# Hybrid decoder step: four samples' weights ahead of two key units, and value fetches between row fetches

## The chip, the core and the metric

One core of a Trainium2 chip runs the kernel. The metric is the device time of one execution in microseconds; lower is better.

## The reference

One layer of a decoder for 256 prompt tokens and 8 sample tokens (width 1024). After a norm and one projection, two mixers run for each group, then a merge, a router and 32 small experts.

```python
# mixer A, sample: top 256 of 2049 keys by an indexer's score, their K and V rows gathered
score = einsum(relu(q_i . k_i), w_i);  sel = top_k(score, 256)
k_sel, v_sel = cache_k_a[phys, off], cache_v_a[phys, off]
o_a = softmax(q . k_sel + bias[bucket(dist)]) @ v_sel
# mixer B, sample: stick-breaking over all 2048 cached keys, 8 heads of 64
z = q . k;  log_keep = log_sigmoid(-z);  after = reverse_cumsum(log_keep) - log_keep
o_b = exp(log_sigmoid(z) + after) @ v
# both mixers also for the prompt, in two blocks of 128 queries; then
h = x + (g_a * (o_a @ w_proj_a) + g_b * (o_b @ w_proj_b)) @ w_out;  out = h + experts(norm(h))
```

## The kernel before

All engines work in a written order; semaphores tie them together. The change lies in the stage in which the samples' mixer B is finished and mixer A runs.

Mixer B of the samples reads K and V caches in 32 units each. A unit is four rows of each of 128 partitions, 1 MB. GpSimd issues each as an indirect DMA (`fetch`, L547 to L550). VectorE multiplies and sums a key unit (`unit(k)`, L1729, 4.6 us). A "used" unit raises `s_kused` or, for values, `s_vused`. Value unit n goes to one of eight slots: from unit 8 on its fetch waits until unit n - 8 is used (`s_vused` at n - 7); units 4 to 7 go to slots of the key ring and wait for the last four key units.

The weights of stick-breaking come for four samples at a time (q = 0, 1). `softplus_keys(q)` scans, `after_keys(q)` on TensorE and `sample_tot(q)` on ScalarE carry the sums across partitions, `later_keys(q)` on VectorE adds them, and `sample_a(q)` on ScalarE takes the exponential into a zeroed pad (`a_pads`, zeroed by GpSimd for q = 0). TensorE's `values(first, units)` (L1015) then takes four matmuls for each unit; unit 0 waits for `sample_a(0)`, unit 16 for `sample_a(1)` and `sample_wide(0)`.

Mixer A of the samples: VectorE writes the list of the selected rows (`list_rows`), and GpSimd fetches 16 blocks of 128 key rows (64 KB each, `got_k`), then 16 of value rows into the same tiles (`got_v`). `turn_got(g)` transposes the key blocks 4g to 4g + 3 on TensorE and ScalarE copies them; `got_v` of a group waits for that transposition. `sample_logits` needs all 16 key blocks, `values_a` all 16 value blocks. Mixer A of the prompt runs between: `prompt_a_scores(i)`, `prompt_a_logits(i)`, ScalarE's `prompt_a_exp(i)` and `prompt_a_values(i, unit)`, which takes value units of mixer B in between its steps. `prompt_b_logits`, `prompt_b_after` and `prompt_b_values` are mixer B of the prompt.

GpSimd's order before: value units 0 to 3, the zeroing, units 4 and 5, key blocks 0 to 7, unit 6, key blocks 8 to 11, unit 7, key blocks 12 to 15, units 8 and 9, value block 0, and then a unit and a value block in turn up to unit 24 and block 15, and units 25 to 31. SP issues the projection weights when 28 value units are used (L483) and the experts' weights behind that.

Of the kernel before, what the change touches and what calls it, by code (L numbers as in the profile page):

```python
# [25 lines left out]
NS = 8  # L26
# [98 lines left out]
def decoder_step(nc, a, out, CONST_AT):  # L125

    ctx = ExitStack()
    with ctx:
# [60 lines left out]
        LIST = 2 * NS  # L189
        got = temp[:, 10240:12288].rearrange("p (x n) -> p x n", x=LIST)  # L190
# [39 lines left out]
        got_row = pads[:, 743:743 + LIST].bitcast(I32)  # L230
# [102 lines left out]
        s_got_k = [sem(f"s_got_k{i}") for i in range(4)]  # L333
# [50 lines left out]
        ka_rows = a["cache_k_a"][0].rearrange("n s h d -> (n s) (h d)")  # L384
# [160 lines left out]
        @block.gpsimd  # L545
        def _(pool):
            def fetch(dst, src, idx, landed):  # L547

                pool.indirect_dma_start(out=dst, out_offset=None, in_=src,  # L549
                                        in_offset=bass.IndirectOffsetOnAxis(ap=idx, axis=0)).then_inc(landed, 16)  # L550

            def fetch_k(k):
                b, u = k // 4, k % 4
                fetch(k_ring[:, u].rearrange("p r n -> p (r n)"), kb_rows, unit_idx[:, u, b:b + 1], s_k[u])

            def fetch_v(n):
                if n >= 8:
                    pool.wait_ge(s_vused, n - 7)
                elif n >= 4:
                    pool.wait_ge(s_kused, 4 * NS - 7 + n)  # L560
                fetch(v_slot(n).rearrange("p r n -> p (r n)"), vb_rows, unit_idx[:, n % 4, n // 4:n // 4 + 1], s_v[n % 8])

            def got_k(g):
                for x in range(4 * g, 4 * g + 4):
                    fetch(got[:, x, :], ka_rows, got_row[:, x:x + 1], s_got_k[g])

            def got_v(x):
                if x % 4 == 0:
                    pool.wait_ge(s_tr, M_GOT + x // 4 + 1)
                fetch(got[:, x, :], va_rows, got_row[:, x:x + 1], s_got_v)  # L570

            pool.wait_ge(s_ms, 1)
            nc.gpsimd.tensor_tensor(rstd, ms, const("half"), ALU.pow).then_inc(s_rstd, 1)
            pool.wait_ge(s_idx, 4)
            pool.wait_ge(s_wa, 16)
            for g in range(2):
                for k in (2 * g, 2 * g + 1):
                    fetch_k(k)
                for b in range(4 * g, 4 * g + 4):
                    fetch(kidx_ring[:, b, :], kidx_rows, page_idx[:, b:b + 1], s_kidx[g])  # L580
            for k in range(4, 4 * NS):
                pool.wait_ge(s_kused, k - 3)
                fetch_k(k)
            pool.wait_ge(s_proj, N_ALL)
            for n in range(4):
                fetch_v(n)
            nc.gpsimd.memset(a_pads[0], 0.0).then_inc(s_apad0, 1)
            fetch_v(4)
            fetch_v(5)
            pool.wait_ge(s_rows, 1)  # L590
            got_k(0)
            got_k(1)
            fetch_v(6)
            got_k(2)
            fetch_v(7)
            got_k(3)
            for n in range(8, 4 * NS):
                fetch_v(n)
                if 9 <= n < 9 + LIST:
                    got_v(n - 9)  # L600

            for n, t in enumerate((0, 2, 1)):
                pool.wait_ge(s_ms2, n + 1)
                nc.gpsimd.tensor_tensor(rstd[:, t:t + 1], ms[:, t:t + 1], const("half")[:, t:t + 1], ALU.pow  # L604
                                        ).then_inc(s_rstd2, 1)

            for t in range(3):
                pool.wait_ge(s_ms3, t + 1)
                nc.gpsimd.tensor_tensor(rstd[:, t:t + 1], ms[:, t:t + 1], const("half")[:, t:t + 1], ALU.pow  # L609
                                        ).then_inc(s_rstd3, 1)  # L610

        @block.tensor
        def _(pe):
# [211 lines left out]
            def turn_got(g):  # L825
                m = M_GOT + g
                pe.wait_ge(s_got_k[g], 64)
                pe.wait_ge(s_trf, m - 1)
                for k in range(4):
                    last = nc.tensor.transpose(PS[:, 2 + m % 2, k * P:(k + 1) * P], got[:, 4 * g + k, :], ident)  # L830
                last.then_inc(s_tr, 1)
# [183 lines left out]
            def values(first, units):  # L1015

                for k in range(first, first + units):
                    b, u, q = k // 4, k % 4, k // 16
                    if k % 16 == 0:
                        pe.wait_ge(s_as, q + 1)  # L1020
                    if k == 16:
                        pe.wait_ge(s_owide, 1)
                    pe.wait_ge(s_v[k % 8], k // 8 * 16 + 16)
                    for r in range(4):
                        last = nc.tensor.matmul(PS[r * 32:(r + 1) * 32, 0, :], a_pad[q][:, b % 4, 4 * u + r, :],  # L1025
                                                v_slot(k)[:, r, :], start=(k % 16 == 0), stop=(k % 16 == 15))
                    last.then_inc(s_vused, 1)
# [8 lines left out]
                last.then_inc(s_tr, 1)  # L1036

            prompt_a_logits(0)
            values(0, 3)
            turn_got(0)  # L1040
            turn_got(1)
            prompt_a_scores(1)
            values(3, 2)
            turn_got(2)
            turn_got(3)
            sample_logits()
            values(5, 1)
            after_keys(1)
            prompt_a_values(0, 6)
            prompt_a_logits(1)  # L1050
            values(10, 2)
            turn_soft()
            prompt_a_turn(0)
            values(12, 2)
            prompt_b_logits(0)
            values(14, 2)
            prompt_a_values(1, 16)
            fold_heads(0)
            prompt_a_turn(1)
# [240 lines left out]
        def _(act):  # L1300
# [113 lines left out]
            def sample_a(q, s_zero):  # L1414
                act.wait_ge(s_zero, 1)
                act.wait_ge(s_ts, q + 1)
                nc.scalar.activation(a_own[q], z_s[:, 4 * q:4 * q + 4, :].rearrange("p b (h r) -> p b r h", r=R), ACT.Exp  # L1417
                                     ).then_inc(s_as, 1)
# [25 lines left out]
            def list_told(m, dst):  # L1444
                act.wait_ge(s_tr, m + 1)
                nc.scalar.copy(dst, PS[:, 2 + m % 2, 0:dst.shape[1]]).then_inc(s_trf, 1)
# [14 lines left out]
            sample_tot(0)  # L1461
            act.wait_ge(s_tr, M_NEW + 1)
            nc.scalar.copy(tmp64, PS[0:64, 2 + M_NEW % 2, 0:NS]).then_inc(s_trf, 1)
            list_told(M_BUCKET, bucketT)
            def turned_got(g):
                m = M_GOT + g
# [70 lines left out]
                                          PS[half, 1 if k == 0 else ACC + 3, :].rearrange("p (c q) -> p c q", c=2))  # L1537
                last.then_inc(s_obT, 1)

            sample_a(0, s_apad0)  # L1540
            sample_ln(1)
            prompt_a_exp(0)
            turned_got(0)
# [132 lines left out]
        def _(dve):  # L1676
# [274 lines left out]
            unit(13 + ROUNDS)  # L1951
            softplus_keys(0)
            list_rows()
            unit(14 + ROUNDS)
            unit(15 + ROUNDS)
            later_keys(0)
            link(nc.vector.tensor_scalar(wi_scaled, wi_rows[:, :, :], float(H ** -0.5 * HD ** -0.5), None, ALU.mult))

            def prompt_a_scores(i):
# [397 lines left out]
```

## Time and profile before

| | us |
|---|---|
| median of 3 runs (667.5 to 670.08) | 667.61 |
| profiled execution | 666.25 |
| its span | 664.4 |
| TensorE busy | 562.7 |
| VectorE busy | 371.5 |
| GpSimd busy | 129.8 |
| ScalarE busy | 136.2 |

The span is the time from the first to the last instruction; the rest of the profiled execution's time lies around it. Busy time of an engine is a share over all stages and tells little of the stage at hand. There the share of the 16 transfer engines and the granted TensorE clock (1.00 is 2.4 GHz, 0.50 is 1.2 GHz) are to be read by stretches.

### The profile page before, as it was taken

To read this page: it belongs to the slowest core of one execution; us is meant where nothing else is said; L and a number is where in the kernel's file an instruction comes from. 1 tells how busy PE (TensorE), PEld (TensorE's weight loads), DVE (VectorE), ACT (ScalarE), POOL (GpSimd) and SP (SyncE) were. 2 spreads that over 40 slices of the span, in tenths; PEclk is the share of its full clock that TensorE was granted. 3 is DMA by queue.
4 is the path that set the end of the run, shared out by engine and by line. 5 is a ranking of instruction groups with operands and counts; after the bars stand their busy time and mean duration, and the time that the engine had idled before them with its cause. 6 is when DMAs were issued, how large, how long until landed. Compare 5 with 4: busy or idle time off the path is not lost.

```text
span 664.4 us, 7517 instructions
## 1 busy us (share of the span) xinstructions
PE 562.7 (85%) x2900; PEld 317.7 (48%) x2900; DVE 371.5 (56%) x679; ACT 136.2 (20%) x267; POOL 129.8 (20%) x116
## 2 busy tenths in 40 slices
PE   3998889989999467988979997797998989788882
PEld 1775567877888424446468445332322323222220
DVE  4069999999999998820423144734342442414124
ACT  3013401115211144451610021110101111010102
POOL 1625441111111877772000000000000000000001
PEclk9999989999999567985999999798999999999997
DMA  8999768798874948999469983469999999999951
GB/s 311 398 357 334 288 235 325 291 402 299 289 281 133 378 153 314 422 423 394 172 163 408 384 340 106 148 220 417 419 420 418 421 420 421 420 420 421 407 233 68
DMA packets 66318, 213.83 MB, mean 322 GB/s; under 512 B 15379, under 2 KB 17955, under 8 KB 58092
## 3 DMA queue, kind: packets, MB, share of 16 engines
q1 hardware_dynamic: 52108, 137.46, 53.2%
q0 software_dynamic: 11392, 73.41, 28.8%
q10 hardware_dynamic: 2784, 2.51, 1.1%
q8 instruction: 21, 0.34, 0.2%
q14 instruction: 13, 0.11, 0.0%
HBM read 208.76 MB, written 4.60 MB: 321 GB/s over the span
## 4 chain that ended last, share of the span: by engine, by line
PE 44%; DVE 24%; SPq 10%; DMA 7%; ACT 6%; issue 5%; POOL 3%; ACTq 1%; DVEq 0%
PE PS L619 7%; SPq L469 7%; DVE arena L1734 6%; PE PS L1185 6%; DVE x_rows L1738 6%; PE PS L1167 5%; PE PS L1080 4%; PE PS L1095 4%; PE PS L1193 3%; DMA arena<-in_w_down 3%; SPq L474 3%; PE PS L1233 3%; DMA arena<-in_w_up 2%; POOL arena L549 2%; POOL temp L549 1%
## 5 line engine op out<-in xcount | busy, mean ns | idle before, releaser
L619 PE MATMUL PS<-xT,arena 128*128 128x264 f32 x608 | 145.6, 399 | 0.8 <-ACT arena L1376 0.5
L619 PEld LDWEIGHTS PS<-xT,arena 128*128 128x128 f32 x608 | 116.8, 195 | 26.4 <-issue 4.7
L1734 DVE TENSOR_TENSOR arena<-arena,x_rows 128x2048 f32<-128x2048 f32 x32 | 73.1, 2283 | 21.2 <-ACT x_rows L1328 21.1
L1738 DVE TENSOR_REDUCE x_rows<-arena 128x32 f32<-128x2048 f32 x32 | 73.2, 2287 | 1.1
L549 POOL DMA_INDIRECT arena<-in_cache_k_b,unit_idx x32 | 44.6, 1395 | 138.9 <-DVE x_rows L1738 134.5
L1193 PE MATMUL PS<-temp 128*128 128x512 f32 (+1 forms) x96 | 48.9, 646 | 12.4 <-DVE temp L2261 8.1
L1185 PE MATMUL PS<-arena,temp 128*32 128x512 f32 x384 | 48.0, 644 | 9.3 <-DMA arena<-in_w_up 4.8
L609 POOL TENSOR_TENSOR small<-small,consts 128x1 f32<-128x1 f32 x3 | 2.6, 868 | 241.2 <-DVE small L2297 241.2
L2237 DVE TENSOR_TENSOR x_rows<-PS,x_rows 128x512 f32<-128x512 f32 (+1 forms) x48 | 32.9, 687 | 24.4 <-PE PS L1193 24.3
L549 POOL DMA_INDIRECT arena<-in_cache_v_b,unit_idx x32 | 34.9, 1090 | 29.6 <-PE PS L1025 13.4
L2261 DVE COPY temp<-PS 128x512 f32<-128x512 f32 x8 | 5.5, 691 | 55.1 <-PE PS L1233 55.1
L1193 PEld LDWEIGHTS PS<-temp 128*128 128x128 f32 (+1 forms) x96 | 12.8, 164 | 48.3 <-DVE x_rows L2237 25.5
L1185 PEld LDWEIGHTS PS<-arena,temp 128*32 128x32 f32 x384 | 12.0, 118 | 40.8 <-issue 32.3
L1233 PE MATMUL PS<-arena,temp 128*32 128x512 f32 x256 | 29.0, 592 | 0.7 <-DMA arena<-in_w_down 0.7
L1095 PE MATMUL PS<-temp,xT 128*128 128x512 f32 x64 | 28.5, 599 | 0.0
L1025 PE MATMUL PS<-arena,xT 128*32 128x512 f32 x128 | 18.1, 685 | 9.2 <-ACT xT L1417 9.2
L1316 ACT COPY arena<-PS 128x264 f32<-128x264 f32 x22 | 8.3, 378 | 84.9 <-PE PS L619 84.9
L2257 DVE TENSOR_TENSOR temp<-PS,temp 128x256 f32<-128x256 f32 x8 | 3.4, 424 | 35.0 <-ACT temp L1628 35.0
L2220 DVE COPY temp<-PS 128x512 f32<-128x512 f32 x8 | 5.5, 691 | 28.0 <-PE PS L1167 28.0
L549 POOL DMA_INDIRECT temp<-in_cache_k_a,pads x16 | 19.1, 1196 | 4.9 <-issue 4.9
L604 POOL TENSOR_TENSOR small<-small,consts 128x1 f32<-128x1 f32 x3 | 1.6, 548 | 92.4 <-DVE small L2074 76.2
L1167 PE MATMUL PS<-rows_vb,temp 128*128 128x512 f32 x32 | 18.9, 675 | 0.7 <-DVE temp L2194 0.7
(374 smaller groups left out, 804.2 us busy)
## 6 DMA issues: line engine op xcount, KB each, us to landing
arena<-in_w_down SPq DMA_DIRECT2D x32, 1024.0 KB, 15.9
arena<-in_w_gate SPq DMA_DIRECT2D x48, 512.0 KB, 13.1
arena<-in_w_up SPq DMA_DIRECT2D x48, 512.0 KB, 13.6
arena<-in_w_in SPq DMA_DIRECT2D x9, 2048.0 KB, 11.3
temp<-in_w_gate SPq DMA_DIRECT2D x12, 512.0 KB, 14.8
temp<-in_w_up SPq DMA_DIRECT2D x12, 512.0 KB, 14.7
temp<-in_w_out SPq DMA_DIRECT2D x1, 4096.0 KB, 15.3
x_rows<-in_x_prompt SPq DMA_DIRECT2D x2, 1024.0 KB
```

What stands on the lines that cost most here:

```text
L469: sp.dma_start(region[:, g * 4 * DE:(g + 1) * 4 * DE], w[e].rearrange("o (p h c) f -> h (o p) (c f)", p=P, h=2)[half]).then_inc(s_second i ...
L549: pool.indirect_dma_start(out=dst, out_offset=None, in_=src, in_offset=bass.IndirectOffsetOnAxis(ap=idx, axis=0)).then_inc(landed, 16)
L619: last = nc.tensor.matmul(PS[0:m, n % 2, 0:T], w[:, k, c0:c0 + m], xT[:, k, :], start=(k == 0), stop=(k == KC - 1))
L1080: last = nc.tensor.matmul(PS[:, bank + c % 2, 0:T], w[:, k, c * P:(c + 1) * P], o[:, k, :], start=(k == 0), stop=(k == 3))
L1095: last = nc.tensor.matmul(PS[:, (6 + 2 * t + n) % 8, :], mixT[:, k, t * P:(t + 1) * P], w_o[:, k, n * 512:(n + 1) * 512], start=(k == 0), ...
L1167: last = nc.tensor.matmul(PS[:, half, :], into[0:n, t, :], x2_rows[t][0:n, half * 512:(half + 1) * 512], start=(t == 0), stop=(t == 2))
L1185: last = nc.tensor.matmul(PS[k * CAP:(k + 1) * CAP, 2, :].rearrange("p (g f) -> p g f", g=2), xgT[:, d, k * CAP:(k + 1) * CAP], both[:, :, ...
L1193: return nc.tensor.matmul(PS[0:n, ACC + 2 + half, :], backT[:, t0:t0 + n], y_sb[:, half, :], start=True, stop=True)
L1233: last = nc.tensor.matmul(PS[k * CAP:(k + 1) * CAP, ACC + half, :], hidT[:, f, k * CAP:(k + 1) * CAP], slots[k][:, w0:w0 + 512], start=(f ...
L1734: nc.vector.tensor_tensor(k_ring[:, u], k_ring[:, u], q_all[:, b % 2:b % 2 + 1, :].to_broadcast([P, 4, H * HD]), ALU.mult).then_inc(s_mul, 1)
L1738: nc.vector.tensor_reduce(z_s[:, b, :].rearrange("p (h r) -> p r h", r=R)[:, 4 * u:4 * u + 4, :], k_ring[:, u].rearrange("p r (h d) -> p r ...
L2237: nc.vector.tensor_tensor(x_rows[0:n, t, cols], PS[0:n, ACC + 2 + half, :], x_rows[0:n, t, cols], ALU.add).then_inc(added, 1)
```

## The change

VectorE runs `later_keys(0)` in front of key units 30 and 31. ScalarE runs `sample_a(0)` in front of its copy of the buckets. GpSimd issues key blocks 0 to 3, then units 6, 8, 9, 7, 10 to 15, each followed by one key block, then key blocks 14 and 15; from unit 16 on value blocks follow, two behind each of units 16 to 19 and one behind each of units 20 to 27. TensorE takes value units 0 to 5 at once, 6 and 7 behind `turn_got(0)`, 8 behind `turn_got(1)` and `prompt_a_scores(1)`, 9 behind `sample_logits`, 10 to 13 within `prompt_a_values(0)`, and 14 and 15 singly behind it.

```diff
--- before.py
+++ after.py
@@ -560,9 +560,8 @@
                     pool.wait_ge(s_kused, 4 * NS - 7 + n)
                 fetch(v_slot(n).rearrange("p r n -> p (r n)"), vb_rows, unit_idx[:, n % 4, n // 4:n // 4 + 1], s_v[n % 8])
 
-            def got_k(g):
-                for x in range(4 * g, 4 * g + 4):
-                    fetch(got[:, x, :], ka_rows, got_row[:, x:x + 1], s_got_k[g])
+            def got_k(x):
+                fetch(got[:, x, :], ka_rows, got_row[:, x:x + 1], s_got_k[x // 4])
 
             def got_v(x):
                 if x % 4 == 0:
@@ -588,16 +587,20 @@
             fetch_v(4)
             fetch_v(5)
             pool.wait_ge(s_rows, 1)
-            got_k(0)
-            got_k(1)
-            fetch_v(6)
-            got_k(2)
-            fetch_v(7)
-            got_k(3)
-            for n in range(8, 4 * NS):
+            for x in range(4):
+                got_k(x)
+            for x, n in enumerate((6, 8, 9, 7, 10, 11, 12, 13, 14, 15)):
                 fetch_v(n)
-                if 9 <= n < 9 + LIST:
-                    got_v(n - 9)
+                got_k(4 + x)
+            got_k(14)
+            got_k(15)
+            for n in range(16, 4 * NS):
+                fetch_v(n)
+                if n < 20:
+                    got_v(2 * n - 32)
+                    got_v(2 * n - 31)
+                elif n < 28:
+                    got_v(n - 12)
 
             for n, t in enumerate((0, 2, 1)):
                 pool.wait_ge(s_ms2, n + 1)
@@ -1036,24 +1039,24 @@
                 last.then_inc(s_tr, 1)
 
             prompt_a_logits(0)
-            values(0, 3)
+            values(0, 6)
             turn_got(0)
+            values(6, 2)
             turn_got(1)
             prompt_a_scores(1)
-            values(3, 2)
+            values(8, 1)
             turn_got(2)
             turn_got(3)
             sample_logits()
-            values(5, 1)
+            values(9, 1)
             after_keys(1)
-            prompt_a_values(0, 6)
+            prompt_a_values(0, 10)
             prompt_a_logits(1)
-            values(10, 2)
+            values(14, 1)
             turn_soft()
             prompt_a_turn(0)
-            values(12, 2)
+            values(15, 1)
             prompt_b_logits(0)
-            values(14, 2)
             prompt_a_values(1, 16)
             fold_heads(0)
             prompt_a_turn(1)
@@ -1461,6 +1464,7 @@
             sample_tot(0)
             act.wait_ge(s_tr, M_NEW + 1)
             nc.scalar.copy(tmp64, PS[0:64, 2 + M_NEW % 2, 0:NS]).then_inc(s_trf, 1)
+            sample_a(0, s_apad0)
             list_told(M_BUCKET, bucketT)
             def turned_got(g):
                 m = M_GOT + g
@@ -1537,7 +1541,6 @@
                                           PS[half, 1 if k == 0 else ACC + 3, :].rearrange("p (c q) -> p c q", c=2))
                 last.then_inc(s_obT, 1)
 
-            sample_a(0, s_apad0)
             sample_ln(1)
             prompt_a_exp(0)
             turned_got(0)
@@ -1951,9 +1954,9 @@
             unit(13 + ROUNDS)
             softplus_keys(0)
             list_rows()
+            later_keys(0)
             unit(14 + ROUNDS)
             unit(15 + ROUNDS)
-            later_keys(0)
             link(nc.vector.tensor_scalar(wi_scaled, wi_rows[:, :, :], float(H ** -0.5 * HD ** -0.5), None, ALU.mult))
 
             def prompt_a_scores(i):
```

## Rows read from the trace of the kernel before

**Rows 1.** Chain that ended last: start us, us, what.

```profile
268.12 0.94 POOL arena L549
...
293.97 7.49 DMA temp<-in_cache_v_a,pads
```

**Rows 2.** Five stretches: columns us, engines' busy (instructions), PEclk, DMA share, GB/s.

```profile
232.00:253.00 21.00, 11.22 (x69) 4.68 (x70) 18.54 (x52) 11.69 (x27) 15.82 (x18) 0.74 0.47 153
253.00:315.00 62.00, 54.63 (x357) 33.41 (x357) 29.69 (x60) 21.49 (x50) 40.02 (x38) 0.81 1.00 406
...
285.00:286.00 1.00, 1.00 (x8) 0.08 (x8) 0.00 (x0) 0.30 (x1) 0.76 (x1) 0.50 0.99 418
...
301.50:314.50 13.00, 13.00 (x43) 10.46 (x44) 0.00 (x0) 1.95 (x5) 2.19 (x3) 0.50 1.01 414
329.90:333.60 3.70, 3.67 (x12) 2.13 (x13) 1.76 (x1) 1.32 (x2) 0.00 (x0) 1.00 1.01 411
```

**Rows 3.** Timeline, VectorE: start us, us, instruction, [idle before it <- releaser].

```profile
224.71 2.28 DVE L1734 TENSOR_TENSOR arena<-arena,x_rows 128x2048 f32<-128x2048 f32 x1
...
233.75 0.20 DVE L1926 TENSOR_TENSOR small<-pads,x_rows 128x32 f32<-128x32 f32 x1
233.98 0.69 DVE L1929 TENSOR_TENSOR x_rows<-x_rows,small 128x512 f32<-128x512 f32 x1
...
270.07 2.48 DVE L1980 SCALAR_TENSOR_TENSOR temp<-PS,temp 128x512 f32<-128x512 f32 x4 [1.12 <-PE PS L931]
```

**Rows 4.** Timeline, GpSimd: four of its issues.

```profile
225.18 2.63 POOL L549 DMA_INDIRECT temp<-in_cache_k_a,pads  x1 [0.30 <-issue]
...
233.88 0.95 POOL L549 DMA_INDIRECT temp<-in_cache_k_a,pads  x1 [0.30 <-issue]
...
250.13 1.24 POOL L549 DMA_INDIRECT temp<-in_cache_k_a,pads  x1 [0.30 <-issue]
...
293.97 2.35 POOL L549 DMA_INDIRECT temp<-in_cache_v_a,pads  x1 [0.31 <-issue]
```

**Rows 5.** Timeline, ScalarE: `sample_tot(0)`, bucket copy, `sample_a(0)` with its table load.

```profile
221.57 0.18 ACT L1412 COPY pads<-PS 128x32 f32<-128x32 f32 x1 [1.49 <-PE PS L783]
...
226.00 0.58 ACT L1446 COPY temp<-PS 128x512 f32<-128x512 f32 x1 [3.43 <-PE PS L821]
234.75 1.28 ACT L1417 ACT_TABLE_LOAD   x1 [8.17 <-DVE x_rows L1929]
236.04 1.07 ACT L1417 ACTIVATE xT<-x_rows 128x512 f32<-128x512 f32 x1
```

**Rows 6.** Timeline, TensorE.

```profile
225.89 2.08 PE L931 MATMUL PS<-arena 64*128 64x128 f32 x16
237.17 5.35 PE L1025 MATMUL PS<-arena,xT 128*32 128x512 f32 x24 [9.20 <-ACT xT L1417]
...
252.94 0.75 PE L830 MATMUL PS<-consts,temp 128*128 128x128 f32 x4 [0.49 <-DMA temp<-in_cache_k_a,pads]
255.19 1.09 PE L840 MATMUL PS<-temp,bias_b 128*64 128x128 f32 x4 [1.50 <-ACT obT L1468]
...
283.49 1.46 PE L961 MATMUL PS<-rows_kva,temp 128*128 128x64 f32 x8 [2.39 <-ACT temp L1507]
...
292.97 1.07 PE L1025 MATMUL PS<-arena,temp 128*32 128x512 f32 x8
...
295.44 2.78 PE L1025 MATMUL PS<-arena,temp 128*32 128x512 f32 x24
301.50 0.68 PE L864 MATMUL PS<-pads,rows_kva 8*128 8x64 f32 x2 [3.27 <-DMA temp<-in_cache_v_a,pads]
302.11 7.00 PE L867 MATMUL PS<-pads,temp 128*128 128x8 f32 x32
```

**Rows 7.** Issues of 250 to 251 and of 251.5 to 252.5 us, us to landing.

```profile
temp<-in_cache_k_a,pads POOLq DMA_INDIRECT x1, 2.8
...
arena<-in_cache_v_b,unit_idx POOLq DMA_INDIRECT x1, 5.4
```

## The prediction, on record before the result

> **What bounds the kernel now.** I read the chain of waits first, then the share of the transfer engines by stretch, then the timelines of GpSimd, VectorE, ScalarE and TensorE between 220 and 342 us, and last the landing times of the indirect fetches.
>
> The reader is to see one stage, from about 225 to 341 us, in which GpSimd issues 32 value units of 1 MB, 16 blocks of key rows and 16 blocks of value rows (64 KB each) one after the other. An issue takes 0.94 us and the next follows 0.30 us later, so one per 1.25 us [rows 4]. The chain runs over these issues from 268 to 294 us and ends in the landing of the last block of value rows, 7.49 us after its issue began [rows 1]. TensorE has reached `values_a` by then: its last value units before it end at 295.44 + 2.78 = 298.2, and it stands 3.27 us until 301.5 [rows 6]. From 232 to 253 us the transfer engines are only 0.47 busy, so 21 x 0.53 = 11 us of their time are lost; from 253 to 315 they are full [rows 2]. The change aims at that gap. But the order in which GpSimd issues also says when the sixteen blocks of key rows are there, and TensorE, which works in a written order, waits for them before `sample_logits`.
>
> **Weights earlier (VectorE, ScalarE).** `later_keys(0)` now stands at 233.75, behind two key units of which the first begins at 224.71 [rows 3]. What it needs, `sample_tot(0)`, is done at 221.57 + 0.18 [rows 5]. So it runs at 224.7 without a wait and takes 0.9 us, and both key units end 0.9 us later; VectorE's work is only reordered and its next step starts as before. On ScalarE `sample_a(0)` moves ahead of the copy at 226.00; its table load of 1.28 us and the activation of 1.07 us, now 234.75 to 237.1 [rows 5], come to 225.7 to 228.1. The copy then runs at 228.1 instead of 226.0; its consumers are VectorE's `prompt_a_logits(0)` (243.9, not late) and `sample_logits`. TensorE finishes `prompt_a_logits(0)` at 225.89 + 2.08 = 228.0, so its first value unit starts at 228.1 instead of 237.17, 9 us earlier [rows 6]. That alone shortens nothing, because another wait stands behind it.
>
> **Fetches reordered (GpSimd).** Counted in issues from 225.18: before, the last block of key rows is the 18th (16 blocks and units 6 and 7) and begins at 250.13 [rows 4]. After, it is the 26th: four blocks, ten pairs of unit and block, two blocks. None of the units 6 to 15 waits for its slot: unit 8 needs one used unit and comes at 236.4, and unit 7 needs the last key unit, done at 234.7, and comes at 241.4. The first four blocks are as before and end at 233.88. From there 21 issues lie ahead of it, 233.88 + 21 x 1.25 = 260.1, 10.0 us later than now.
>
> Its landing: before, with the engines half empty, 2.8 us after the issue, 252.9 [rows 7]. After, ten units and twelve blocks stand in the queue from 235.3 on, with no idle engine between. A unit is 1.05 MB, at about 420 GB/s 2.5 us; a block some 0.3 us (from 253 to 315 us 23 units and 16 blocks passed: 23 x 2.5 + 16 x 0.3 = 62.3 [rows 2]). 10 x 2.5 + 12 x 0.3 = 28.6, so 263.9, and 1 us for completion: 264.9. Ends: 262.9 if it lands 2.8 us after its issue as now, and 266.5 if it has the 7.5 us of the last value rows less their long issue.
>
> The Trainium skill, "DMA: Bandwidth & Descriptors", section "Anatomy of one DMA", gives a DMA issued from GpSimd as 2.0 us and its bytes over 436 GB/s; for 64 KB an estimate of 2.15 us, near the 2.8 us measured in the half empty stretch, far from the 7.49 us in the full one. By that formula alone the block would land at 262.3 and the sum below would be 2.6 us less.
>
> **What that does to TensorE.** Values(6, 2) and `turn_got(1)` wait for unit 7 and block 7 until about 248; `prompt_a_scores(1)` then ends at about 252.5, when ScalarE is free for it anyway, so this costs nothing. `turn_got(3)` runs at 264.9 instead of 252.94. With 0.75 us for its transposes, 0.6 us for the copy and the signals, `sample_logits` starts at 266.6 instead of 255.19 [rows 6]: 11.4 us late (9.4 to 13 by the ends above).
>
> Behind it all is serial. Five value units and `prompt_a_values(0)` lie between `sample_logits` and `prompt_a_logits(1)`, before and after alike; VectorE waits for the latter today, 1.12 us [rows 3], then forms logits and maximum, ScalarE's exponentials follow, and TensorE waits 2.39 us for ScalarE's copies at 283.49 [rows 6]. Four units fewer stand between `sample_logits` and that point now, but TensorE has slack there, and so the 3.8 us of them (1.92 us for two) buy nothing. So TensorE arrives at `values_a` at 298.2 + 11.4 = 309.6.
>
> The value rows: GpSimd's unit 17 needs ten used units, and the tenth is computed after `sample_logits`, at 272; GpSimd could have issued at 265.1 and stands 7 us, and the engines run dry about as long, so most of the 11 us gained is lost again. The last block of value rows now stands behind unit 27, before behind unit 24; unit 27 needs twenty used units, the last of which ends at 292.97 + 1.07 + 11.4 = 305.4 [rows 6]. Unit 27 is issued at 305.6, the block at 306.9. The engines have caught up by then, so unit 27 lands after 5.4 us [rows 7], at 311, and the block with it. `values_a` starts at 311.0: 3.3 us of wait shrink to 1.4, and the stage is 9.5 us late (7.8 to 11.4 by the two ends).
>
> **The clock.** Before, TensorE's granted clock is 0.50 (1.2 GHz) from the wait at 298.2 through `values_a` and `prompt_b_after(0)`, 13.0 us of work; `prompt_b_after(1)`, the same matmuls, takes 3.7 us at 1.00 (2.4 GHz) [rows 2] where the first took 6.5. With the wait cut to 1.4 us, the clock may stay up for a part. All of it would give 3.5 us (half of the 7.0 of `values_a`) and 2.8 us, 6.3 in all; nothing is the other end. The wait of 2.39 us before 283.49 was followed by a fall (0.50 at 285) [rows 2, 6], and `values_a` streams eight columns a matmul [rows 6], light work, so I take 1.5 us, nearer to nothing.
>
> The Trainium skill, "TensorE: Matmul & The Clock Gate", section "HAM oscillation", advises to finish the matmuls of a group before the next wait for a transfer, so that the engine stays at 2.4 GHz; the change does that with six units and then two. By that rule the whole 6.3 us would come back, the rival "clock" below. The trace agrees in so far as the clock was down behind the two waits of 2.39 and 3.27 us [rows 2, 6]; no row shows what a wait of 1.4 us does.
>
> **Sum.** The rest of the stage, the weights of the projections (issued when 28 units are used) and the experts follow TensorE, so the delay passes to the end. 666.25 us of the profiled execution + 9.5 - 1.5 = 674.25. The median of the three runs, 667.61, lies 1.36 above the profiled one: **675.5 us**.
>
> **Rivals.**
> *Clock:* all as above, but the clock stays at 2.4 GHz through `values_a` and `prompt_b_after(0)`. For it speaks the shorter wait, against it the light matmuls. +9.5 - 6.3: 670.8 us.
> *Catch-up (the other side):* the engines' 11 us are won and `sample_logits` is not late, since the key rows pass the units in the queue. It decides from a delay of `sample_logits` under 3.3 us, the present wait at `values_a`. Then only the issues count: the last value rows are three later, 293.97 + 3.75 = 297.7, land 2.8 us later at 300.5, 1.0 us earlier than now, and the clock stays up: 667.6 - 1.0 - 6.3 = 660.3 us. Against it: the 26th issue cannot begin before 260.1.
> *Weights not early:* the table load or the zeroing of the pad holds `sample_a(0)`, the first value unit still starts at 237, and unit 8 waits for its slot until 239, 2.5 us longer than forecast. Everything behind is later by that, 678.1 us. The zeroing stands ahead of the key rows on GpSimd, which speaks against it.
> *Queue:* key rows at the late end and unit 27 later: +11.4 and no clock: 679.0 us.
>
> **How the numbers follow.** Forecast 0.62, clock 0.14, catch-up 0.07, weights not early 0.05, queue 0.12. The range goes from the early end of the delay with the full clock (+7.8 - 6.3, 669.1) to +11.4 with none (679.0): 669.5 to 679. About 0.5% (3.3 us) is what a measurement of this kernel can tell from no change. Faster by more: the catch-up case, 0.06. Within: the rest of it and the half of the clock case under 670.9, with the lowest edge of the forecast, 0.09. Slower: 0.85.
>
> **What would show it.** Right: the first value unit on TensorE at 228; the last key-row issue at about 260 and `turn_got(3)` waiting on it until 264 to 266; a gap of some 7 us in GpSimd's issues behind unit 16; `sample_logits` 9 to 13 us later; the wait ahead of `values_a` under 2 us. Wrong: `sample_logits` before 259, or transfer engines full from 235 to 300 without a gap.

## The result, and the profile after

The changed kernel takes 683.97 us (median of 4 runs, 682.37 to 684.74), the kernel before beside it 667.56 us (4 runs, 665.04 to 670.08). The ratio is 1.024 with an interval of 1.020 to 1.029: slower by 16.4 us. I had forecast 675.5 us and a range up to 679.0. The direction was right, the size was too small by half (some 8 us of the 16.4), and the time lies outside the range.

The profiled execution took 684.74 us with a span of 682.9 us and a mean granted clock of 0.915. Lines of the changed kernel stand 3 lines lower from the reordered part on (L1025 is now L1028, L864 is L867). This execution was 1.83 us ahead at the first value fetch on GpSimd, before anything of the change acts (212.22 against 214.05 us). So a delay within the stage is the time after, plus 1.83, minus the time before.

First the five columns of stretches, as in [rows 2], of the changed kernel: start:end, us, busy time of PE, PEld, DVE, ACT and POOL with instructions, PEclk, DMA share, GB/s.

```profile
232.00:253.00 21.00, 9.27 (x52) 4.36 (x56) 17.19 (x51) 9.82 (x26) 16.12 (x17) 0.67 0.96 376
253.00:315.00 62.00, 42.92 (x293) 25.02 (x285) 29.04 (x59) 19.49 (x44) 37.82 (x37) 0.77 0.78 286
```

The gap is filled as it was meant to be: the transfer engines go from 0.47 to 0.96, a gain of 21 x 0.49 = 10.3 us. But the stretch behind goes from 1.00 to 0.78, a loss of 62 x 0.22 = 13.6 us. TensorE's busy time there falls from 54.63 to 42.92 us. The empty time has moved, and grown.

TensorE's timeline, in the form of [rows 6], shows where:

```profile
226.36 5.52 PE L1028 MATMUL PS<-arena,xT 128*32 128x512 f32 x40 [0.18 <-ACT xT L1420]
...
246.45 1.93 PE L1028 MATMUL PS<-arena,xT 128*32 128x512 f32 x8 [8.17 <-DMA arena<-in_cache_v_b,unit_idx]
...
257.61 1.12 PE L833 MATMUL PS<-consts,temp 128*128 128x128 f32 x4 [3.79 <-DMA temp<-in_cache_k_a,pads]
...
263.61 1.12 PE L833 MATMUL PS<-consts,temp 128*128 128x128 f32 x4 [4.88 <-DMA temp<-in_cache_k_a,pads]
265.49 1.08 PE L843 MATMUL PS<-temp,bias_b 128*64 128x128 f32 x4 [0.77 <-ACT obT L1472]
...
293.27 1.97 PE L964 MATMUL PS<-rows_kva,temp 128*128 128x64 f32 x8 [3.08 <-ACT temp L1511]
...
308.43 2.78 PE L1028 MATMUL PS<-arena,temp 128*32 128x512 f32 x24
...
315.49 0.68 PE L867 MATMUL PS<-pads,rows_kva 8*128 8x64 f32 x2 [4.28 <-DMA temp<-in_cache_v_a,pads]
316.10 7.00 PE L870 MATMUL PS<-pads,temp 128*128 128x8 f32 x32
...
356.14 2.02 PE L1083 MATMUL PS<-oaT,arena 128*128 128x264 f32 x8 [1.25 <-ACT obT L1540]
```

The wait of 9.20 us for the first weights is gone, and the first unit starts at 226.36. In its place stand 8.17 us for unit 6, 3.79 for key rows and 4.88 for the last key rows. `sample_logits` starts at 265.49 + 1.83 = 267.3, 12.1 us later than at 255.19. The wait at `values_a` has not shrunk from 3.27 us, it is 4.28.

GpSimd's timeline, in the form of [rows 4], has the stall behind unit 16, and the issues of units 24 to 27 with the last value-row block (the last key-row block is issued at 258.88):

```profile
271.64 0.94 POOL L549 DMA_INDIRECT arena<-in_cache_v_b,unit_idx  x1 [8.08 <-PE PS L1028]
...
297.41 0.94 POOL L549 DMA_INDIRECT arena<-in_cache_v_b,unit_idx  x1 [2.67 <-PE PS L1028]
...
301.93 0.94 POOL L549 DMA_INDIRECT arena<-in_cache_v_b,unit_idx  x1 [2.32 <-PE PS L1028]
...
305.30 0.94 POOL L549 DMA_INDIRECT arena<-in_cache_v_b,unit_idx  x1 [1.18 <-PE PS L1028]
...
307.79 1.50 POOL L549 DMA_INDIRECT arena<-in_cache_v_b,unit_idx  x1 [0.30 <-issue]
...
309.60 1.49 POOL L549 DMA_INDIRECT temp<-in_cache_v_a,pads  x1 [0.30 <-issue]
```

The chain of waits between 258 and 316 us (start, us, what), which before ran from 268 us on over GpSimd's issues alone [rows 1], now goes through the whole serial part of the stage:

```profile
258.88 4.68 DMA temp<-in_cache_k_a,pads
...
279.86 0.83 DVE temp L1983 x2
...
287.27 2.95 ACT temp L1503 x11
...
293.27 1.97 PE PS L964 x8
...
304.00 1.04 PE PS L1028 x8
...
305.30 0.94 POOL arena L549
...
309.60 5.84 DMA temp<-in_cache_v_a,pads
315.49 0.68 PE PS L867 x2
```

It reads as one story: last key rows, `turn_got(3)`, `sample_logits`, five units with `prompt_a_values(0)`, `prompt_a_logits(1)`, VectorE's logits and maximum, ScalarE's exponentials, `prompt_a_values(1)`, the used slot, unit 26, unit 27, the last value rows, `values_a`.

### The profile page after: what moved, and what is told of

The parts are those of the page before. It is cut to its first block, busy times and chain, and to the rows that moved or that the text cites. A ratio compares the mean times of both kernels' runs of the same rounds, so it can differ in the third digit from the quotient of the medians.

```text
span 682.9 us, 7517 instructions
## 1 busy us (share of the span) xinstructions
PE 571.3 (84%) x2900; PEld 323.2 (47%) x2900; DVE 371.5 (54%) x679; ACT 136.6 (20%) x267; POOL 129.2 (19%) x116
## 4 chain that ended last, share of the span: by engine, by line
PE 50%; DVE 15%; SPq 9%; DMA 9%; ACT 5%; POOL 5%; issue 4%; ACTq 1%; DVEq 0%
PE PS L622 11%; SPq L469 7%; PE PS L1188 6%; PE PS L1170 5%; PE PS L1083 4%; PE PS L1098 4%; DVE arena L1737 4%; DVE x_rows L1741 3%; PE PS L1196 3%; DMA arena<-in_w_down 3%; POOL arena L549 3%; SPq L474 3%; PE PS L1236 3%; DMA arena<-in_w_up 2%; DMA arena<-in_cache_v_b,unit_idx 2%
## 5 line engine op out<-in xcount | busy, mean ns | idle before, releaser
L622 PE MATMUL PS<-xT,arena 128*128 128x264 f32 x608 | 143.3, 394 | 1.1 <-ACT arena L1379 0.7
L1028 PE MATMUL PS<-arena,xT 128*32 128x512 f32 x128 | 17.9, 663 | 12.0 <-DMA arena<-in_cache_v_b,unit_idx 11.8
## 6 DMA issues: line engine op xcount, KB each, us to landing
arena<-in_w_in SPq DMA_DIRECT2D x9, 2048.0 KB, 11.2
temp<-in_w_gate SPq DMA_DIRECT2D x12, 512.0 KB, 13.7
temp<-in_w_up SPq DMA_DIRECT2D x12, 512.0 KB, 13.6
```

Of the source, the lines that this page charges most:

```text
L622: last = nc.tensor.matmul(PS[0:m, n % 2, 0:T], w[:, k, c0:c0 + m], xT[:, k, :], start=(k == 0), stop=(k == KC - 1))
```

## The experiments

The theory after the result (A): the late key rows hold the serial chain back, the late value rows add a part of their own, and TensorE's clock, which falls at the new waits, adds a third part. The rivals: the early weights do the harm, or the order of the units on TensorE does (four fewer units before `prompt_a_values(1)`), or nothing but the clock. The first four kernels, and those at the end, ran where the kernel before took 668 us (the record names chips 13 and 9); a group between them ran where it took 682 to 683 us (chips 11 and 0), and is read against its own runs of the kernel before.

**Early weights alone.** The kernel before with only the two moves:

```diff
+            sample_a(0, s_apad0)
             list_told(M_BUCKET, bucketT)
...
-            sample_a(0, s_apad0)
             sample_ln(1)
...
+            later_keys(0)
             unit(14 + ROUNDS)
             unit(15 + ROUNDS)
-            later_keys(0)
```

> The kernel before with the moves on VectorE and ScalarE alone (later_keys(0) and sample_a(0) early); orders of GpSimd and TensorE as before. Theory A (the order of fetches costs, the early weights cost nothing): first value unit at about 228 instead of 237, end of the stage where it was, 667.6 us within 2. Rival B (the early start itself costs, because TensorE stands longer afterwards and its clock falls in other places): 670 us or more, sample_logits unmoved but more time at 0.50 between 240 and 315 us.

Measured: 668.55 us (10 runs) beside 668.93 of before, ratio 0.9988 (0.996 to 1.0016). TensorE's timeline of it:

```profile
228.63 4.05 PE L1025 MATMUL PS<-arena,xT 128*32 128x512 f32 x24 [0.19 <-ACT xT L1417]
...
240.38 1.12 PE L830 MATMUL PS<-consts,temp 128*128 128x128 f32 x4 [2.81 <-DMA temp<-in_cache_k_a,pads]
...
255.58 0.62 PE L840 MATMUL PS<-temp,bias_b 128*64 128x128 f32 x4 [1.57 <-ACT obT L1469]
...
282.68 1.97 PE L961 MATMUL PS<-rows_kva,temp 128*128 128x64 f32 x8 [2.89 <-ACT temp L1508]
...
296.22 1.08 PE L1034 MATMUL PS<-consts,x_rows 128*128 128x32 f32 x8
```

The wait of 9.2 us goes, waits for the key rows take its place, and `sample_logits` stands where it was (255.58 against 255.19). Harmless and worthless by itself, as forecast. One thing in this profile matters further on: `prompt_a_values(1)` lasts 13.5 us here (282.68 to 296.22, granted clock 0.63) and not the 10.5 us of the profile before (283.49 to 293.97), although TensorE's order is that of before.

**Orders alone.** The changed kernel with those two moves taken back (the diff above, reversed).

> The changed kernel with later_keys(0) and sample_a(0) back in their old places. Theory A: the whole cost of 16 us stays, plus up to 2.5 us because unit 8 waits for its slot until the first unit is used at 239: 684 to 687 us. Rival B: most of the 16 us goes away, under 676 us.

Measured: 688.31 us (4 runs), ratio 1.031 (1.025 to 1.037), 4.3 us over the changed kernel. The intervals overlap, so the 4.3 us are likely rather than settled. `sample_logits` starts at 268.73. So the orders carry the whole loss, and the early weights are, if anything, a help within them. Its `prompt_a_values(1)` is the shorter one, 10.8 us, and yet TensorE waits 3.92 us at `values_a`:

```profile
297.23 1.97 PE L964 MATMUL PS<-rows_kva,temp 128*128 128x64 f32 x8 [2.69 <-ACT temp L1510]
...
308.06 1.08 PE L1037 MATMUL PS<-consts,x_rows 128*128 128x32 f32 x8
...
316.24 0.68 PE L867 MATMUL PS<-pads,rows_kva 8*128 8x64 f32 x2 [3.92 <-DMA temp<-in_cache_v_a,pads]
```

**Key rows first again.** The changed kernel with the key-row blocks where they stood before; TensorE's order and the value rows stay changed.

```diff
-            for x in range(4):
+            for x in range(8):
                 got_k(x)
-            for x, n in enumerate((6, 8, 9, 7, 10, 11, 12, 13, 14, 15)):
+            fetch_v(6)
+            for x in range(8, 12):
+                got_k(x)
+            fetch_v(7)
+            for x in range(12, 16):
+                got_k(x)
+            for n in range(8, 16):
                 fetch_v(n)
-                got_k(4 + x)
-            got_k(14)
-            got_k(15)
```

> The changed kernel with GpSimd's key blocks as before (0 to 7, unit 6, 8 to 11, unit 7, 12 to 15, then units 8 to 15); everything else changed. Theory A (the key rows' place in the queue makes sample_logits 12 us late, and the rest follows): turn_got(3) at about 253, sample_logits at 255, last value rows some 10 us earlier, 668 to 673 us. Rival C (the place of the value rows, behind unit 27 and its wait for used units, sets the time whatever the keys do): 678 us or more.

Measured: 676.56 us (4 runs), ratio 1.0126 (1.0072 to 1.0181): 7.4 us under the changed kernel, with the intervals apart. More was expected. Its timeline says why:

```profile
251.28 1.93 PE L1031 MATMUL PS<-arena,xT 128*32 128x512 f32 x8 [4.50 <-DMA arena<-in_cache_v_b,unit_idx]
...
257.99 1.07 PE L1031 MATMUL PS<-arena,xT 128*32 128x512 f32 x8 [1.27 <-DMA arena<-in_cache_v_b,unit_idx]
260.90 0.62 PE L846 MATMUL PS<-temp,bias_b 128*64 128x128 f32 x4 [0.82 <-ACT obT L1475]
...
308.74 0.69 PE L870 MATMUL PS<-pads,rows_kva 8*128 8x64 f32 x2 [5.89 <-DMA temp<-in_cache_v_a,pads]
```

`sample_logits` comes back only to 260.90, since TensorE's new order puts units 6 to 8 in front of it, and two of them are awaited here (another cost of the change, some 5 us, which the late key rows cover in the changed kernel). The wait at `values_a` grows to 5.89 us: the faster chain meets the same late value rows.

**Value rows earlier.** The changed kernel, last value-row block behind unit 23 instead of 27:

```diff
-                if n < 20:
+                if n < 24:
                     got_v(2 * n - 32)
                     got_v(2 * n - 31)
-                elif n < 28:
-                    got_v(n - 12)
```

> The changed kernel with the last value block behind unit 23 instead of 27 (two blocks behind each of units 16 to 23). Theory A: TensorE still reaches values_a at 311 (its own clock), the wait of 4.3 us there goes, and with it perhaps the fall of the clock: 676 to 680 us. Rival C: under 674 us.

Measured: 679.17 us (4 runs), ratio 1.0162 (1.0106 to 1.0219), 4.8 us under the changed kernel. The two intervals overlap at their edges (the changed kernel's begins at 1.020), but no run of the one reaches the other's (677.25 to 679.71 against 682.37 to 684.74 us). The wait is gone, while `sample_logits` stays late:

```profile
267.76 1.09 PE L841 MATMUL PS<-temp,bias_b 128*64 128x128 f32 x4 [0.77 <-ACT obT L1470]
...
313.57 0.43 PE L865 MATMUL PS<-pads,rows_kva 8*128 8x64 f32 x2
```

**Both given back.** The two last diffs together.

> The changed kernel with both orders given back: key blocks as before, the last value block behind unit 23. Early weights and TensorE's new grouping of value units stay. If the two costs add up (7.4 and 4.8 us found apart), 671 to 673 us; if they overlap, since without the late key rows the wait for the value rows was longer (5.9 us), 668 us or less; if TensorE's grouping costs by itself (units 6 to 9 awaited ahead of key and logit work), it stays above 670 us with sample_logits at 261 instead of 255.

> The same kernel as e8_keys_first_rows_23 once more: there every kernel, the one before too, was some 12 us slower and spread over 15 us, with stretches in which TensorE stood for instructions. Expected as there: 671 to 673 us if the two costs add up, 668 or less if they overlap, above 670 with sample_logits at 261 if TensorE's grouping of value units costs by itself.

> Both orders of GpSimd given back, TensorE's grouping and the early weights kept. The two costs add up: 12 us under after_again, 4 us over the kernel before. They overlap or take the clock with them: 14 us or more under after_again, within 2 us of the kernel before.

Measured in three rounds, all in the group in which the kernel before took 682 to 683 us: 686.01, 683.87 and 680.7 us (10 runs each); ratios 1.002 (0.9971 to 1.007), 1.0026 (0.9988 to 1.0064), 0.9984 (0.9941 to 1.0027). All three include 1. In the third round the changed kernel itself ran beside it, and took 9.8 us more, less than the 12 or 14 expected. Given back together, GpSimd's two orders remove all of the loss that this group shows; whether the two costs add up or overlap, it doesn't tell.

**Both kernels again, unedited,** to have their times and profiles in that group.

> The changed kernel once more, as a base for e5c: 1.024 times the kernel before where no instruction stalls occur; where they do, both theories allow less, since the stalls fall in the same stretch in which it waits for rows.

> The kernel before once more, with a profile: ratio 1.00. If the job is one of the slower ones, TensorE, ScalarE or VectorE stand for instructions between 245 and 320 us, 12 us in all or more; if not, values_a starts at 301 as on record.

Measured: the changed kernel 690.5 us (10 runs), ratio 1.0096 (1.0045 to 1.0147); the kernel before 683.62 us, ratio 1.0034 (0.9971 to 1.0098). In this group the change costs 7 us and not 16: the kernel before has itself lost 16.1 us against its first runs (683.62 against 667.56), the changed kernel only 6.5. The profile of that run of the kernel before shows stalls which [rows 6] don't have:

```profile
267.36 1.08 PE L840 MATMUL PS<-temp,bias_b 128*64 128x128 f32 x4 [5.71 <-issue]
...
299.97 1.97 PE L961 MATMUL PS<-rows_kva,temp 128*128 128x64 f32 x8 [5.77 <-issue]
...
317.66 0.43 PE L864 MATMUL PS<-pads,rows_kva 8*128 8x64 f32 x2
```

TensorE stands 5.3 us (in four pieces before 257 us), 5.71 and 5.77 us, and the profile names no releaser ("issue"). The four pieces lie within one value unit, where the written order awaits nothing. The two longer stalls are, by the written order, waits for copies of ScalarE: they end 0.15 and 0.05 us after such copies end (267.21 and 299.92 us). ScalarE had itself stood before them. In front of the first of the two the chain has

```profile
260.83 4.32 another core or an unknown queue
```

and in front of the second ScalarE's timeline has idle time of 2.03 and 0.87 us with the releaser "remote". The first profile has neither in this stretch. TensorE comes to `values_a` 15 us later (317.66 less 1.20, by which this execution was behind at the first value fetch, against 301.50), after the value rows have landed, and has no wait there. The changed kernel, profiled beside it, stands 8.24 us by "issue" in front of unit 6, where it waited 8.17 us for that unit's transfer in its first profile: a stall in the place of a wait costs nothing. That hides part of what the change costs.

**The clock, by added matmuls.** Matmuls on constants, put in front of waits to keep TensorE working; they are added work whose results nothing reads (three of them are the x6 in the trace below). In the changed kernel at three places, seven in all:

```diff
             prompt_b_logits(0)
+            fill(2)
             prompt_a_values(1, 16)
...
+                    if i and g == 0:
+                        fill(2)
...
+            fill(3)
             values_a()
```

> The changed kernel with seven added matmuls of 512 columns whose results are not used: two behind prompt_b_logits(0), two before the first wait for copied weights in prompt_a_values(1), three before values_a; TensorE stands still there otherwise. Theory D (about 3 us of the loss at prompt_a_values(1) is the lower clock behind its waits, and the clock also stays down through values_a and prompt_b_after(0)): the granted clock stays at 1.00 from 286 to 330 us, prompt_a_values(1) is 3 us shorter, values_a and prompt_b_after(0) up to 6 us: 675 to 679 us. Rival E (the clock follows the waits but hides behind transfers): 682 us or more.

> The same kernel as e5_after_fill once more, for the same reason. Theory D: 675 to 679 us, granted clock 1.00 from 286 to 330 us. Rival E: 682 us or more.

> The changed kernel with the seven added matmuls. Theory D (the lower clock costs 3 us in prompt_a_values(1) and up to 6 us in values_a and prompt_b_after(0)): 5 to 9 us under after_again. Rival E (what is won hides behind the wait for value rows): within 2 us of after_again.

Measured: 689.68 us at 1.0013 (0.9959 to 1.0066), 686.44 at 1.0082 (1.0038 to 1.0126), 683.65 at 1.006 (1.0021 to 1.0099), 10 runs each. Beside the third round the changed kernel took 690.5 us at 1.0096 (1.0045 to 1.0147). The medians differ by 6.9 us, the ratios by 0.4% with intervals that overlap: by the times a gain isn't settled. The added work has a price of its own, too (next experiment). TensorE's timeline in the third round:

```profile
297.88 1.10 PE L966 MATMUL PS<-rows_kva,temp 128*128 128x64 f32 x8 [1.44 <-ACT temp L1519]
...
310.97 2.84 PE L1045 MATMUL PS<-consts 128*128 128x512 f32 x6
...
315.79 0.43 PE L867 MATMUL PS<-pads,rows_kva 8*128 8x64 f32 x2 [1.98 <-DMA temp<-in_cache_v_a,pads]
316.15 6.32 PE L870 MATMUL PS<-pads,temp 128*128 128x8 f32 x32
```

and its stretches, of `prompt_a_values(1)` and of `values_a`, with the same of the changed kernel in the second fence, and the first of the two of the kernel before in the third:

```profile
297.80:306.90 9.10, 9.02 (x73) 5.41 (x74) 0.84 (x2) 7.21 (x8) 4.52 (x5) 1.00 0.57 212
...
315.80:322.50 6.70, 6.70 (x35) 6.63 (x36) 0.00 (x0) 0.00 (x0) 0.21 (x1) 0.58 0.99 390
```

```profile
293.20:307.10 13.90, 13.83 (x74) 8.46 (x74) 0.98 (x2) 7.21 (x8) 6.51 (x8) 0.63 0.82 300
...
315.50:322.90 7.40, 7.40 (x34) 7.28 (x35) 0.00 (x0) 0.00 (x0) 0.00 (x0) 0.50 0.82 320
```

```profile
283.50:294.10 10.60, 10.60 (x73) 6.10 (x74) 0.96 (x2) 7.12 (x7) 7.85 (x10) 0.84 1.02 426
```

The same 74 matmuls (as the trace counts them; it shows one matmul of the program as two, as with the x6 above) take 9.0 us at a granted clock of 1.00 (2.4 GHz) and 13.8 us at 0.63. The kernel before takes 10.6 us for this step, at 0.84. So the clock of this step is worth 3.2 us between the two profiled executions. It isn't shown that the change sets it, for other profiles don't sort by the order of the units. From the step's first matmul to the next step's, and granted clock over it, where the kernel before took 668 us:

| TensorE's order | `prompt_a_values(1)` |
|---|---|
| before, six units in front | 10.5 us at 0.84 (kernel before), 13.5 at 0.63 (early weights alone), 8.9 at 1.00 and 11.7 at 0.75 (the last two kernels below, in their runs beside 667.69) |
| changed, two units in front | 13.7 us at 0.63 (changed kernel), 10.8 at 0.81 (orders alone), 11.6 at 0.75 (key rows first), 13.7 at 0.62 (value rows earlier) |

With the added matmuls the three rounds have 8.9, 10.5 and 8.9 us, the changed kernel beside the third 11.2 at 0.78. So added work in front seems to help, but the full clock came once without it.

At `values_a` the added work brings little: it starts at the full clock and has 0.58 over its length, 6.32 us instead of 7.00.

**The same at `values_a` in the kernel before.** `fill(3)` in front of `values_a`, nothing else.

> The kernel before with three such added matmuls in the 3.3 us wait before values_a. Theory D: values_a and prompt_b_after(0) run at 1.00, up to 6.3 us less: 661 to 665 us. Rival F (values_a is too light and the clock falls within it, so that prompt_b_after(0) is slow as before): 1 to 3 us less at most, 665 to 667 us.

> The same kernel as e6_before_fill once more. Theory D: 661 to 665 us. Rival F (the clock falls within values_a): 665 to 667 us.

Measured: 686.96 us at 1.0082 (1.0035 to 1.0128) and 687.93 at 1.0083 (1.0048 to 1.0118), 12 runs each: slower. It was to fill a wait of 3.27 us, but neither profile has a wait at `values_a`, so 2.84 us of added matmuls come on top. The ratio stands for 5.6 us (in the second round 3.3 at least), and what the rest is isn't known. As a test of the clock it says nothing.

**Value rows earlier in the kernel before.** If the last value rows are a cost of their own, they should be so before the change as well. Blocks 13 to 15 behind unit 22, instead of behind 22, 23 and 24:

```diff
-                if 9 <= n < 9 + LIST:
+                if 9 <= n < 22:
                     got_v(n - 9)
+                if n == 22:
+                    for x in (13, 14, 15):
+                        got_v(x)
```

> The kernel before with value blocks 13, 14 and 15 all behind unit 22 (before: behind 22, 23 and 24). Theory G (the last value block sets the start of values_a, until TensorE's own arrival at 298.2): the wait of 3.3 us goes, 3 us less and perhaps the clock: 661 to 665 us. Rival: units 20 to 22 or a later wait take its place, 667 us.

> The same kernel as e7_before_rows_22 once more. Theory G: the wait of 3.3 us before values_a goes, 661 to 665 us. Rival: another wait takes its place, 667 us.

> The kernel before with value blocks 13 to 15 behind unit 22. Where no instruction stalls occur: the wait of 3.3 us before values_a goes, ratio 0.990 to 0.996. Where they occur, TensorE arrives after the rows anyway: 0.997 to 1.002.

Measured: 683.67 us at 1.0017 (0.9983 to 1.0051) and 683.63 at 0.9955 (0.991 to 1.0) in the slower group, where the kernel before, profiled once, had no wait at `values_a`, and 665.75 us at 0.9954 (0.9924 to 0.9984), 12 runs, beside 667.69, where its first profile has the wait. There:

```profile
282.27 1.10 PE L964 MATMUL PS<-rows_kva,temp 128*128 128x64 f32 x8 [2.81 <-ACT temp L1510]
...
291.17 1.08 PE L1037 MATMUL PS<-consts,x_rows 128*128 128x32 f32 x8
...
295.74 1.06 PE L1028 MATMUL PS<-arena,temp 128*32 128x512 f32 x8 [1.17 <-DMA arena<-in_cache_v_b,unit_idx]
296.74 0.43 PE L867 MATMUL PS<-pads,rows_kva 8*128 8x64 f32 x2
```

The wait of 3.27 us is gone; 1.17 us for a unit comes in its place.

**That and the early weights.** The last diff together with the first.

> The same with later_keys(0) and sample_a(0) early as in the change. The early weights alone were worth nothing (0.9988), so within 0.3% of e7c; under 0.995 would be a version that beats both kernels.

Measured: 663.58 us (12 runs, 660.81 to 666.69) beside 667.69, ratio 0.9922 (0.9891 to 0.9954). It beats both kernels. Its timeline:

```profile
297.79 0.43 PE L867 MATMUL PS<-pads,rows_kva 8*128 8x64 f32 x2
298.15 3.95 PE L870 MATMUL PS<-pads,temp 128*128 128x8 f32 x32
```

No wait, and `values_a` in 3.95 us instead of 7.00: in this execution the granted clock there was 0.94. In the kernel with the value rows alone it took 6.29 us, also without a wait in front, so that the wait is gone doesn't settle the clock. Against the kernel with the value rows alone the intervals overlap, so a gain from the early weights on top isn't shown.

## Why the prediction was wrong in size

**Right.** The first value unit was forecast at 228.1 and came at 226.36 + 1.83 = 228.2. The last key-row issue was forecast at 260.1 and began at 260.7; `turn_got(3)` at 264.9 and ran at 265.4; `sample_logits` 11.4 us late and was 12.1; GpSimd's stall behind unit 16 some 7 us and was 8.08. That the early weights alone shorten nothing is shown by their own run (0.9988). That the key rows' place is a cause is shown by 7.4 us won when it is undone; and that the place of the value rows is another, by 4.8 us.

**The step that failed first: "So TensorE arrives at `values_a` at 298.2 + 11.4 = 309.6".** It arrived at 311.21 + 1.83 = 313.0. Up to the start of `prompt_a_values(1)` the delay was handed on almost unchanged (293.27 + 1.83 - 283.49 = 11.6 us). But I took the step's length from the trace of before. There it lasts from 283.49 to 293.97, 10.5 us; after, from 293.27 to 306.95, 13.7 us, with the clock at 0.50 (1.2 GHz) from 290 to 303. 11.6 + 3.2 = 14.8 us. Why the clock was lower is open. The four units that no longer stand in front don't decide it: with six in front the same step took 8.9 to 13.5 us in four profiles, with two 10.8 to 13.7 in four. The sum should have had this step as a range and not as one figure.

**The second: "Unit 27 is issued at 305.6, the block at 306.9 [...] `values_a` starts at 311.0".** On the scale of the trace before, the block was issued at 309.60 + 1.83 = 311.4, 4.5 us later, and landed at 317.3. `values_a` was 15.8 us late instead of 9.5, and its wait 4.28 us instead of 1.4: the term was too small by 6.3 us. Units 24 to 26 each wait until TensorE has used a unit within `prompt_a_values(1)` (2.67, 2.32 and 1.18 us); unit 27 no longer waits. So the place that counts is that of unit 18, whose use releases unit 26. In the trace of before it is used at 292.0:

```profile
290.94 1.06 PE L1025 MATMUL PS<-arena,temp 128*32 128x512 f32 x8
```

With the 11.4 us that makes 303.4, and it was 305.04 + 1.83 = 306.9: 3.5 of the 6.3 us come from the longer step, whose delay GpSimd's queue hands on. The other 2.8 us are the queue itself. I let unit 27 follow unit 19 at once, and its landing stand for the block's. In fact unit 26, block 14, unit 27 (1.50 us instead of 0.94) and the last block are issued one after the other, 4.6 us from unit 18's use to the last issue, and the block lands 5.84 us after that, while TensorE has 6.2 us of work left: a wait of 4.3. It hardly hangs on the clock: with the orders alone, where the step took 10.8 us, the wait is 3.92.

**The third: "so I take 1.5 us" of clock.** The wait wasn't shorter, and `values_a` took 7.00 us, as before and as in every profile with a wait of 2.9 us or more in front of it. `prompt_b_after(0)` gave back 0.7 us (5.8 against 6.5), and the matmuls of `prompt_b_values(1)` at 350 to 355 us ran for the most part at 0.50 and cost 1.7 us. So the clock behind the wait cost 1.0 us instead of giving 1.5. The clock rival counted only on what could be won; that other work behind could run at the low level wasn't among my cases.

**The rest.** At L1083 the delay is 356.14 + 1.83 - 341.13 = 16.8 us, near the 16.4 of the medians. Behind it the profiled pair parts by another 3.5 us, some 0.8 of it before 453 us, and the rest in the last experts (a step of gate and up of 6.59 against 5.37 us, the last transfer of the down weights of 19.44 against 17.98 us). No experiment bears on that, and I take it for no part of the change. For the profiled pair the account is: forecast 674.25, + 6.3 (value rows and `prompt_a_values(1)`), + 2.5 (clock), + 3.5 (experts), - 1.8 (the lead at the start) = 684.75, measured 684.74. That it closes shows that nothing is left out, not that each part is an effect of the change: the terms are read from this one pair. The two ends of the delay didn't follow from their own figures either: `sample_logits` late by 9.4 and 13 gives 7.5 and 11.1 us by the same working, not 7.8 and 11.4. That moves neither the forecast nor its side of the range's edge.

Shown, then: both of GpSimd's orders cost, and together they account for all of the loss that the slower group shows. Where the kernel before takes 668 us, 7.4 + 4.8 = 12.2 of the 16.4 us come back singly; the two were not tried together there. TensorE's new order has waits that show once the key rows are early (units 7 and 8 awaited 4.50 and 1.27 us in front of `sample_logits`), but it was never run by itself, so that rival is not excluded where the kernel before takes 668 us. Open, too: how much of the 16.4 us the clock is. The profiled pair has 3.2 us of it in one step, the other profiles scatter by more than that, and the times don't decide it. The Trainium skill, "TensorE: Matmul & The Clock Gate", section "HAM oscillation", advises to group matmuls so that waits don't break them up. The change did group six units, and the clock from 232 to 253 us was 0.67, against 0.74 before [rows 2]: grouping the work in front of a wait that is only moved did not keep the engine at 2.4 GHz here. Of the Trainium skill, "DMA: Bandwidth & Descriptors", section "Anatomy of one DMA", the estimate for 64 KB was 2.15 us; the last key rows took 4.7 us from issue to landing with units ahead of them, and the last value rows 5.8.

## What to carry to other kernels

In a queue that issues one transfer every 1.25 us, a small transfer that a serial chain awaits costs by its place: count the issues up to it before filling an idle stretch with large ones. Once something is late, don't carry a TensorE step's length over from one trace as if it were fixed: the same 74 matmuls took 8.9 to 13.7 us here by the granted clock alone, so give such a step a range, or profile more than once. And where fetches wait for used slots, find the last one that really waits, and count every issue between it and the transfer that is awaited. The cheap repair here was to move what is needed earlier ahead of what is needed later: two small blocks moved forward by one and two units, with the early weights, gave 663.6 us, where filling the idle engines cost 16.

## What the runs showed that was not expected

In one group of runs TensorE stood 5.3, 5.7 and 5.8 us with no releaser but "issue", all between 250 and 300 us beside the indirect fetches, and the same kernel took 683 instead of 668 us. Behind the two longer stalls stood ScalarE, which awaited "another core or an unknown queue". That group ran on other chips than the rest; the cause isn't known.

The 32 light matmuls of `values_a` (8 columns each) are the same in every kernel, and how long they take goes with the wait in front of them. Behind a wait of 2.9 us or more they took 7.00 us in all six profiles (before, changed, changed again, orders alone, key rows first, and one with added matmuls), behind waits of 1.0 to 2.0 us 5.20 to 6.32 us in three. Without a wait they took 3.90 to 6.29 us in eleven profiles: each time a part of them ran above 0.50, and only twice (3.90, 3.95) nearly all at the full clock.
